# Attention of the later pairs of tiles, moved from a phase of its own to beside the expert gathers

## What is computed

```
q, k, v = heads of h @ w_in                        # 8 query heads, 2 key heads, 64 wide
y_att  = softmax(q k_all / 8) v_all                # latents: over context and latents, 768 keys
yc_att = softmax(qc kc / 8) vc                     # context, layer 0 only: 256 keys
y_sc, y_hy = a short and a long convolution
x = x + gt1 * (sum_b sigmoid(gate_b) * (y_b @ w_b)) @ w_o
h2 = rmsnorm(x) * (1 + sc2) + sh2
# experts (peer): per token 8 heads, 16 experts each out of 16384
q = h2 @ wq; top 16 of the sums of two score lists -> e, g = softmax
x = x + gt2 * sum_k g_k * gelu(u[e_k] . h2) * v[e_k]
```

## Time and profile before

| | us |
|---|---|
| median of 3 runs | 5218.66 (5212.62 to 5221.26) |
| the profiled execution | 5216.02, its span 5214.2 |
| TensorE / VectorE / ScalarE / GpSimd busy | 3760.7 / 3536.1 / 2117.9 / 2401.2 |
| layer 0's attention phase, first to next phase's first matmul | 197.5 to 308.3 |
| layer 1's | 3512.7 to 3600.6 |
| the three `phase_later_beside` | about 1034 to 1724, 1790 to 2474, 3806 to 4488 |

### The profile page before, as it was taken

How to read it: one execution, slowest core, us unless ns; L and a number is a source line. 1 busy time by engine, 2 the same in 40 slices (tenths; PEclk the granted TensorE clock), 3 DMA queues, 4 the chain that set the end, 5 groups by cost and what they waited for, 6 DMA issues and landing times. The chain is left out here.

```text
span 5214.2 us, 66316 instructions
## 1 busy us (share of the span) xinstructions
PE 3760.7 (72%) x22176; PEld 2005.4 (38%) x22176; DVE 3536.1 (68%) x7189; ACT 2117.9 (41%) x5510; POOL 2401.2 (46%) x1707
## 2 busy tenths in 40 slices
PE   6899878767776577767587688668867766655554
PEld 2678337733333143333122255256833333211111
DVE  7532444487887778877557778764478888777776
ACT  5332103444444444444343445225444445434343
POOL 5112005566665466655333355212756665444443
PEclk8999888888888788888798899889988888777776
DMA  6011104599999999999999899832599999999998
GB/s 245 20 37 45 41 16 152 179 402 411 396 411 398 391 411 410 405 402 385 397 397 359 346 358 387 345 146 91 164 373 416 410 398 407 401 420 413 412 418 337
DMA packets 276195, 1636.17 MB, mean 314 GB/s; under 512 B 30212, under 2 KB 44612, under 8 KB 103564
## 3 DMA queue, kind: packets, MB, share of 16 engines
q0 software_dynamic: 184320, 1342.26, 63.1%
q1 hardware_dynamic: 91532, 289.66, 15.2%
HBM read 1609.68 MB, written 22.12 MB: 313 GB/s over the span
## 5 line engine op out<-in xcount | busy, mean ns | idle before, releaser
L531 POOL DMA_INDIRECT arena<-in_uv,arena x1280 | 1504.7, 1176 | 1680.1 <-PE psum L576 1197.9
L576 PE MATMUL psum<-arena 64*64 64x512 f32 x10240 | 1592.6, 749 | 867.8 <-ACT arena L555 842.4
L691 DVE SCALAR_TENSOR_TENSOR arena<-arena 128x1024 f32<-128x1024 f32 x1280 | 1747.5, 1365 | 643.1 <-DMA arena<-in_uv,arena 587.7
L1569 PE MATMUL psum<-view_at,view_at 128*128 128x256 f32 (+1 forms) x7968 | 1257.8, 313 | 139.2 <-POOL view_at L267 74.9
L1569 PEld LDWEIGHTS psum<-view_at,view_at 128*128 128x128 f32 x7968 | 1104.6, 199 | 555.0 <-issue 383.6
L267 POOL TENSOR_TENSOR view_at<-view_at,view_at 128x1024 fp32r<-128x1024 f32 x376 | 800.9, 2139 | 931.1 <-ACT view_at L360 589.6
L576 PEld LDWEIGHTS psum<-arena 64*64 64x64 f32 x10240 | 388.6, 157 | 1729.0 <-ACT arena L555 1143.5
L544 ACT ACTIVATE arena<-arena 128x1 f32<-128x1 f32 x1280 | 256.2, 200 | 1804.6 <-DVE arena L691 1764.9
L555 ACT ACTIVATE arena<-arena 128x64 f32<-128x64 f32 x1280 | 445.3, 348 | 88.0 <-PE psum L576 46.5
L548 ACT ACTIVATE arena<-arena 128x1 f32<-128x1 f32 x1280 | 377.1, 295 | 46.4
L360 ACT ACTIVATE view_at<-view_at 128x1024 fp32r<-128x1024 f32 x320 | 284.3, 890 | 211.6 <-DMA view_at<-in_w_in 114.5
(11 more groups left out here) (273 smaller groups left out, 3519.5 us busy)
## 6 DMA issues: line engine op xcount, KB each, us to landing
view_at<-in_w_in SPq DMA_DIRECT2D x180, 512.0 KB, 7.8
view_at<-in_w_mod SPq DMA_DIRECT2D x48, 1024.0 KB, 12.0
view_at<-in_w_br SPq DMA_DIRECT2D x120, 256.0 KB, 4.8
view_at<-in_w_out SPq DMA_DIRECT2D x40, 512.0 KB, 6.5
view_at<-in_wq SPq DMA_DIRECT2D x40, 512.0 KB, 8.5
arena<-in_uv,arena POOLq DMA_INDIRECT x1280
arena<-mod_rows SPq DMA_DIRECT2D x13, 512.0 KB, 9.3
arena<-in_keys SPq DMA_DIRECT2D x40, 128.0 KB, 8.6
```

The source lines that it names most:

```text
L531: nc.gpsimd.indirect_dma_start(out=self.slots[i % self.ring], out_offset=None, in_=self.table, in_offset=bass.IndirectOffsetOnAxis(ap=self ...
L576: last = nc.tensor.matmul(self.c.psum[tokens, at:at + 512], self.diag[rows, k % 4], self.slots[k % self.ring][rows, D + h * 512:D + (h + 1 ...
L691: nc.vector.scalar_tensor_tensor(out=self.junk, in0=self.slots[i % self.ring][:, 0:D], scalar=1.0, in1=self.h2_turned if i % 2 else self.h ...
L1569: last = nc.tensor.matmul(c.psum[:, at + lo:at + hi], a[:, k], b[:, k, lo:hi], start=(k == 0 and i == 0), stop=(k == kt - 1 and i == 2))
```

## The change

`phase_attention` keeps only tiles 0 and 1, and stores queries of the later tiles, all keys and all values to DRAM. A new phase, `phase_attention_beside`, stands in front of each `phase_later_beside`: it loads queries, keys and values of its two tiles, computes their attention in single-head units beside 76 gathers (68 for the context), and stores the output where `phase_later_beside` reads it. The later phase gets what is left: gathers 76 to 236 and 328 to 492. `phase_first` stores two branches in place of three.

The new phase has 80 steps: 4 leading, then 4 for each of 16 units (8 heads, two tiles), and 12 for the tail. A unit's parts stand at these lags from its first step: scores 0, maxima 3, Exp 4, division and turning 5, copies 8; for each head the values at 7 after its second unit's start, the kept output at 10.

```diff
-def phase_attention(c, layer, full, lay):
+def attention_kept(nc, layer, width):
+    return [nc.dram_tensor(f"later_{name}{layer}", (P, *shape), F32).ap()
+            for name, shape in (("q", (PAIRS, width)), ("k", (KV_HEADS, T_ALL)), ("v", (NT, P)))]
+def phase_attention(c, layer, lay, stores):
-    groups = [(pair, qs, range(NT)) for pair in range(PAIRS) for qs in ((0, 1), (2, 3))]
-    if full:
-        groups += [(pair, (4, 5), range(NT_LAT, NT)) for pair in range(PAIRS)]
+    groups = [(pair, (0, 1), range(NT)) for pair in range(PAIRS)]
...
+            for dst, src in stores:
+                sp.dma_start(dst, src).then_inc(stored, 16)
+            sp.wait_ge(stored, 16 * len(stores))
...
+def phase_attention_beside(c, n_keys, experts, first, last, kept, y_kept):
+    LEAD, EACH, TAIL = 4, 4, 12
+    n_steps = LEAD + EACH * n_units + TAIL
+    share = Share(experts, first, last, steps=n_steps)
...
+        def _(sp):
+            for dst, src, landed in ((qT, q_kept, q_in), (kT[:, :, 0:width], k_kept[:, :, skip:], k_in),
+                                     (vK[:, 0:n_keys], v_kept[:, NT - n_keys:], v_in)):
+                sp.dma_start(dst, src).then_inc(landed, 16)
+            sp.wait_ge(y_done, HEADS)
+            sp.dma_start(y_kept, yT).then_inc(stored, 16)
+            sp.wait_ge(stored, 16)
...
+        def _(pe):
+            for i in range(n_steps):
+                share.tensor(pe, i)
+                if (u := unit(i, 0)) is not None:
+                        pe.wait_ge(exped, u)
+                    for lo, hi in ((0, min(512, width)), (512, width)):
+                            last = nc.tensor.matmul(c.psum[:, lo:hi], qT[rows(u), u // 4, q], kT[rows(u), kv(u), lo:hi],
+                if (u := unit(i, 5)) is not None:
+                    pe.wait_ge(normed, u + 1)
+                if (h := head(i, 7)) is not None:
+                    pe.wait_ge(turned_kept, each * (2 * h + 2))
...
+        def _(act):
+            for i in range(n_steps):
+                share.scalar(act, i)
+                if (u := unit(i, 4)) is not None:
+                    act.wait_ge(maxed, u + 1)
+                    nc.scalar.activation(prob[u % 2][:, 0:width], c.psum[:, 0:width], ACT.Exp, bias=nmax[:, u % 4:u % 4 + 1],
+                                         accum_out=rsum[:, u % 4:u % 4 + 1]).then_inc(exped, 1)
+                if (u := unit(i, 8)) is not None:
+                    for j, piece in enumerate(pieces):
+                        act.wait_ge(turned, each * u + j + 1)
...
-                    [(h_kept, c.hT[:, :, later])] + [(ys_kept[br], lay.ys[br][:, :, later]) for br in range(3)])
+                    [(h_kept, c.hT[:, :, later])] + [(ys_kept[br], lay.ys[br][:, :, later]) for br in (1, 2)])
...
-        phase_later_beside(c, 0, LAST_LATENTS, experts, 0, group - 20, of([h_kept], 0), of(ys_kept, 0))
+        phase_attention_beside(c, NT, experts, 0, 76, of_q(0), of(ys_kept, 0)[0])
+        phase_later_beside(c, 0, LAST_LATENTS, experts, 76, group - 20, of([h_kept], 0), of(ys_kept, 0))
         phase_experts(c, experts, group + 4)
-        phase_later_beside(c, 0, CONTEXT, experts, group + 4, 2 * group - 20, of([h_kept], 1), of(ys_kept, 1))
+        phase_attention_beside(c, NT_CTX, experts, group + 4, group + 72, of_q(1), of(ys_kept, 1)[0])
+        phase_later_beside(c, 0, CONTEXT, experts, group + 72, 2 * group - 20, of([h_kept], 1), of(ys_kept, 1))
```

More of the change, by code:

```diff
@@ L1428, in phase_attention @@
         ring = SplitRing(c, ph, conv_blocks(c, layer)[:0 if lay.apart else 4])
+        stored = ph.sem("later_stored")
         def kv(pair):
@@ L3166, in build @@
         phase_qkv(c, 0, True, lay)
-        phase_attention(c, 0, True, lay)
+        later = slice(GROUP_W, T_ALL)
+        att_kept = attention_kept(nc, 0, T_ALL - GROUP_W)
+        phase_attention(c, 0, lay, list(zip(att_kept, (lay.qT[:, :, later], lay.kT, lay.vK))))
         phase_conv_branches(c, 0)
@@ L3172, in build @@
                 phase_long_conv(c, length, order, lay, Share())
-        later = slice(GROUP_W, T_ALL)
         h_kept = nc.dram_tensor("later_h0", (P, KD, T_ALL - GROUP_W), F32).ap()
@@ L3177, in build @@
         phase_first(c, 0, First(c, lay), experts,
-                    [(h_kept, c.hT[:, :, later])] + [(ys_kept[br], lay.ys[br][:, :, later]) for br in range(3)])
+                    [(h_kept, c.hT[:, :, later])] + [(ys_kept[br], lay.ys[br][:, :, later]) for br in (1, 2)])
         of = lambda a, i: [x[:, :, i * GROUP_W:(i + 1) * GROUP_W] for x in a]
         group = GROUP_TILES * experts.per_tile
-        phase_later_beside(c, 0, LAST_LATENTS, experts, 0, group - 20, of([h_kept], 0), of(ys_kept, 0))
+        of_q = lambda i: [att_kept[0][:, :, i * GROUP_W:(i + 1) * GROUP_W]] + att_kept[1:]
+        phase_attention_beside(c, NT, experts, 0, 76, of_q(0), of(ys_kept, 0)[0])
+        phase_later_beside(c, 0, LAST_LATENTS, experts, 76, group - 20, of([h_kept], 0), of(ys_kept, 0))
         phase_experts(c, experts, group + 4)
-        phase_later_beside(c, 0, CONTEXT, experts, group + 4, 2 * group - 20, of([h_kept], 1), of(ys_kept, 1))
+        phase_attention_beside(c, NT_CTX, experts, group + 4, group + 72, of_q(1), of(ys_kept, 1)[0])
+        phase_later_beside(c, 0, CONTEXT, experts, group + 72, 2 * group - 20, of([h_kept], 1), of(ys_kept, 1))
         latents = NT_LAT * experts.per_tile + 8
@@ L3188, in build @@
         phase_qkv(c, 1, False, lay, moves)
-        phase_attention(c, 1, False, lay)
         later = slice(GROUP_W, L_LAT)
+        att_kept = attention_kept(nc, 1, L_LAT - GROUP_W)
+        phase_attention(c, 1, lay, list(zip(att_kept, (lay.qT[:, :, later], lay.kT, lay.vK))))
         h_kept = [nc.dram_tensor(f"later_h1_{x}", (P, KD, L_LAT - GROUP_W), F32).ap() for x in ("high", "low")]
@@ L3195, in build @@
                     [(kept, h.bitcast(F32)[:, :, later]) for kept, h in zip(h_kept, (lay.hT_high, lay.hT_low))]
-                    + [(ys_kept[br], lay.ys[br][:, :, later]) for br in range(3)])
-        phase_later_beside(c, 1, LAST_LATENTS, experts, 0, group - 20, h_kept, ys_kept)
+                    + [(ys_kept[br], lay.ys[br][:, :, later]) for br in (1, 2)])
+        phase_attention_beside(c, NT, experts, 0, 76, att_kept, ys_kept[0])
+        phase_later_beside(c, 1, LAST_LATENTS, experts, 76, group - 20, h_kept, ys_kept)
         phase_experts(c, experts, experts.n_all)
```

79 lines of the change are left out of this document (added).

## The result

The changed kernel is slower: 5236.05 us (median of 7 runs, 5232.78 to 5246.13) against 5216.69 (7 runs, 5212.62 to 5221.26), a ratio of 1.0042 with a 95% interval of 1.0032 to 1.0052. A second set of runs gave 1.0041 (1.0026 to 1.0056). The forecast was 5175 us, a ratio of 0.992.

A forecast was written before the change was run, and what follows sets the result against it. Bytes at about 407 GB/s were taken to bound the kernel beside gathers, engine chains outside. From 5216.0 us, -103 + 14.5 + 11.7 + 22 + 12 = -43 gave 5173, about 5175 as median; forecast 5155 to 5195, range 5132 to 5214.

The forecast's parts named there:

- What bounds the kernel: Whole kernel: beside expert gathers, bytes over about 407 GB/s; outside them, a chain of TensorE, VectorE, ScalarE, TensorE.
- Removed, 103 us: First attention phases and stores: 59.4 us less in layer 0, 40.8 in layer 1, 3 from one stored branch less.
- The hand-over forecast for 248.9: Layer 0's shortened attention phase hands over to the next at 248.9 where that started at 308.31, saving 59.4 us.
- 3 was taken and 3.9 allowed: First phase after the convolutions, one branch less stored: TensorE's wait for a weight shrinks by 3 us, between 0 and 3.9.
- The merge, 22 us: Later pairs' merges beside 160 gathers instead of 236: TensorE at 85%, DMA at 401 instead of 407 GB/s, 22 us lost.
- the boundaries, 11.7: Starts of the three added phases: 3.9 us each, 11.7 us together, from 0 to twice that.
- Bytes, 14.5 us: Added loads and stores of the three new attention phases: 5.9 MB, 14.5 us, up to twice that.
- The attention beside, 12 us: New attention beside 76 (68) gathers: every engine fits; 2% of 201 + 179 + 201, 12 us lost, from 0 to 60.
- a count of slots: TensorE's wait at the values: 14 us of transfers in flight, sums resume after 7.5 us, 3 to 4 us to spare.
- The upper bound of 20 us a phase: Attention beside the gathers: at most 20 us lost per phase, if half of the slot margin's misses show.
- Rival B: Attention beside the gathers: ScalarE, 82% busy, becomes the engine waited for; 10 to 20 us a phase, 5203 us; chance 0.10.
- Sum: All terms for the whole kernel: -103 + 14.5 + 11.7 + 22 + 12 = -43 us.

The follow-up runs named there:

- run 8: The changed kernel with run 7's edits and Tanh in place of Exp (no softmax in the later tiles): 0.9911 of the kernel before, 5165.7 us.
- run 1: The kernel before with only the later pairs' merges moved beside fewer gathers, the other gathers alone in own phases, attention unmoved: 1.0063 of before, 5238.95 us.
- run 6: The changed kernel with only lags altered: maxima 2, Exp 3, division 4, turning 6, copies 7, values 8, kept output 9: 0.9931 of the kernel before, 5177.6 us.
- run 4: The changed kernel with Tanh in place of Exp in the attention beside the gathers, so fewer table loads and no softmax there: 1.0009 of the kernel before.
- run 7: The kernel of run 6 with the values of two heads done in one go and one kept output for both: 0.9926 of the kernel before, 5177.0 us.

## Why the prediction was wrong

- **What bounds the kernel** (bytes beside the gathers, chains outside): right. Work taken out of the chain was paid in full, and run 8 runs at the bytes' 201 and 179 us.
- **Removed, 103 us**: 108 measured, 66.4 in layer 0 (forecast 59.4 + 3) and 41.4 in layer 1 (40.8). The hand-over forecast for 248.9 in layer 0 came at 248.57; what is over stands behind it, 6.7 us where 3 was taken and 3.9 allowed:

```profile
248.57 11.80 PE L1577 MATMUL psum<-view_at,view_at 128*128 128x512 f32 x62 [1.17 <-PEq L167]
```

- **The merge, 22 us, and the boundaries, 11.7**: run 1 has both together at 20 to 45 us. Right as a sum; one was not separated from the other. The reason given for the 22 us did not come: the merges ran at 393 to 400 GB/s as forecast, but TensorE was busy 73% to 76% of them and not 85%, with a granted clock of 0.87 and 0.88. In the middle of the gates it was 74%:

```profile
1300.00:1600.00 300.00, 223.12 (x1588) 138.43 (x1588) 244.61 (x473) 138.84 (x381) 213.22 (x139) 0.90 0.98 393
```

  So that the size fits is in part luck.
- **Bytes, 14.5 us**: not contradicted. Run 8's stretches lie within 2 us of the time by bytes.
- **The attention beside, 12 us, bounded by 60**: here it failed. 80 us were lost. The step is "a count of slots ... holds with 3 to 4 us to spare". I had seen that TensorE waits at the values for copies of one step later, and priced it. The count had sums resuming after 7.5 us; the trace has 12.9 from the end of one batch to the start of the next. The 5.4 us between them are three things that the count had not. The wait was 6.7 us and not 4.7, for the experts' own Exp stands ahead of the unit's with two more table loads (1054.13 to 1057.12 above). The values ran at the low clock after the wait, 4.7 and not 2.8 us. And the next unit's scores, 1.5 us, stand between the values and the sums. Nor was it one place at risk: the trace has such a wait at all 24 heads (0.3 to 6.7 us), and at the seven between 1000 and 1160 the sums stood still for 8.0 to 13.3 us. In run 6 TensorE waits at the values of none. The upper bound of 20 us a phase came from no row.
- **Rival B** had the place and the sign of the loss (DMA below 0.95 with GpSimd waiting for TensorE), at 10 to 20 us a phase; some 26 came. But its cause, ScalarE's load, is a fifth of it (run 4), and order is most of the rest: run 6 gave back 61 of the 80 us by lags alone. At 0.10 its chance was too low: an in-order wait for a later step of another engine is no matter of averages.
- **Sum**: -108 + 27 (by run 1's medians) + 14.5 + 80 = +13.5 against +19 measured; with 33 us for run 1, by its ratio, it is +19.5. With the order mended, the kernel is at 5177.6 and 5173.3, where 5175 was forecast. That is another kernel than the one forecast, and even there the attention stretches lose 18 us beside their bytes (592 - 559 - 14.5) where 12 was taken.

## What to carry to other kernels

When work is woven step by step beside a queue that must not run dry, write down for each wait the step in which the maker makes it, on the maker's own list; a user in the same or an earlier step can stall its engine in every round (here at every head), and with it whatever stands behind it on that engine (here the sums that free the gathers' slots). Busy shares of 60% to 73% say nothing about that, and neither does a margin worked out for one place. Shifting lags costs nothing in work and was worth 1.1% here; later values or an earlier Exp alone gave 0.65% and 0.1%.

## What the runs showed of the hardware

- A wait of 6.6 us on TensorE (granted clock 1.00 before it, 0.79 over it) was followed by 0.58 for the next 4.7 us, and twelve matmuls took 4.76 us in place of 2.80. In the changed kernel's 1000 to 1160 all seven values took 4.5 to 5.4 us after waits of 3.6 to 6.7 us; with the lags apart, seven of eight took 2.80.
- One head's values alone (12 matmuls, 2.80 us in run 6) took as long as two heads' in turn, each to its own half of the output's partitions (24 matmuls, 2.81 us in run 7): the second head added 0.01 us.
- A switch of ScalarE's table cost 1.28 us in the row and no drain beside it (Exp followed the load 0.02 us later), as in the earlier trace rows; with 90 loads less some 17 us were gained in the changed kernel (run 4), and 11 by the medians, 15 by the stretches, with the order mended (run 8).
